# The last attention on tiles of 32 tokens by four heads, with its operands turned through memory

## The reference

```python
q, k, v, gate = jnp.split(proj, [2048, 2048 + 256, 2048 + 512], axis=-1)
q = rope(rms_norm_2(q.reshape(b, s, 32, 64), q_norm_w), pos)
k = rope(rms_norm_2(k.reshape(b, s, 4, 64), k_norm_w), pos)
o = swa_sinks(q, k, v, sinks)      # scale 1/8, keys t-127 .. t, a sink in the softmax
return (o * jax.nn.silu(gate)) @ w_out
```

## Time and profile before

| | us |
|---|---|
| median of 3 runs | 1880.02 (1879.96 to 1880.33) |
| the profiled execution | 1879.77 |
| its span in the trace | 1878.0 |
| PE busy | 1872.9 |
| DVE busy | 1246.1 |
| ACT busy | 991.1 |

### The profile page before, as it was taken

The page is one execution under the profiler, slowest core; times in us unless marked ns, Lnnn a source line. Parts: engine busy times, 40 slices in busy tenths (PEclk is TensorE's granted clock), DMA queues, the critical chain, the costliest instruction groups (busy, mean ns, idle before and its releaser), DMA issues.

```text
span 1878.0 us, 22471 instructions
## 1 busy us (share of the span) xinstructions
PE 1872.9 (100%) x8531; PEld 1543.7 (82%) x8531; DVE 1246.1 (66%) x1861; ACT 991.1 (53%) x1370; POOL 37.6 (2%) x88
## 2 busy tenths in 40 slices
PE   9999999999999999999999999999999999999999
PEld 7888888888888888888888888888888888877777
DVE  6676566776666556665466776765776666777775
ACT  6677554554444344443444455564565555466653
POOL 0001000000000000000000000000000000111100
PEclk9999999999999999999999999999999999999999
DMA  9767764786666666666666696666666677655665
GB/s 324 205 194 179 207 181 152 217 254 196 192 193 194 194 192 191 192 198 192 191 196 195 204 281 196 194 191 190 190 200 194 194 238 235 174 174 175 182 196 171
DMA packets 212363, 375.97 MB, mean 200 GB/s; under 512 B 14672, under 2 KB 35968, under 8 KB 212256
## 3 DMA queue, kind: packets, MB, share of 16 engines
q1 hardware_dynamic: 211008, 371.78, 65.9%
q0 software_dynamic: 816, 2.11, 0.8%
q10 hardware_dynamic: 432, 0.66, 0.1%
HBM read 361.89 MB, written 12.60 MB: 199 GB/s over the span
## 4 chain that ended last, share of the span: by engine, by line
PE 99%; DMA 0%; SPq 0%; DVE 0%; ACT 0%; DVEq 0%; issue 0%
PE g L1225 32%; PE g L1227 32%; PE g L1226 32%; PE m L1159 1%; PE ob L1304 0%; PE m L1286 0%; DMA raw<-in_w_in 0%; PE m L1386 0%; PE m L1284 0%; PE ob L1307 0%; PE m L1271 0%; PE ob L1372 0%; PE m L1316 0%; PE m L1337 0%; PE g L1213 0%; PE g L1212 0%
## 5 line engine op out<-in xcount | busy, mean ns | idle before, releaser
L1696 DVE TENSOR_TENSOR wl<-raw,wh 128x1024 fp32r<-128x1024 f32 (+1 forms) x660 | 802.6, 1217 | 552.7 <-ACT wh L1416 549.4
L1416 ACT ACTIVATE wh<-raw 128x1024 fp32r<-128x1024 f32 (+1 forms) x661 | 695.3, 1053 | 730.9 <-PE g L1227 724.3
L1225 PE MATMUL g<-wh,xh 128*128 128x512 f32 x1886 | 741.1, 393 | 0.3 <-DVE wl L1696 0.3
L1227 PE MATMUL g<-wh,xl 128*128 128x512 f32 x1886 | 734.4, 389 | 0.0
L1226 PE MATMUL g<-wl,xh 128*128 128x512 f32 x1886 | 734.1, 389 | 0.0
L1225 PEld LDWEIGHTS g<-wh,xh 128*128 128x128 f32 x1886 | 354.1, 188 | 78.5 <-issue 3.9
L1227 PEld LDWEIGHTS g<-wh,xl 128*128 128x128 f32 x1886 | 354.0, 188 | 74.0
L1226 PEld LDWEIGHTS g<-wl,xh 128*128 128x128 f32 x1886 | 354.2, 188 | 71.9
L1225 PE MATMUL g<-wh,mh 128*128 128x512 f32 x732 | 287.1, 392 | 0.0
L1227 PE MATMUL g<-wh,ml 128*128 128x512 f32 x732 | 285.0, 389 | 0.0
L1226 PE MATMUL g<-wl,mh 128*128 128x512 f32 x732 | 284.9, 389 | 0.0
(11 more groups left out here) (193 smaller groups left out, 769.5 us busy)
## 6 DMA issues: line engine op xcount, KB each, us to landing
raw<-in_ev_w_in SPq DMA_DIRECT2D x128, 512.0 KB, 3.9
raw<-in_w_in SPq DMA_DIRECT2D x92, 512.0 KB, 4.2
raw<-in_w_gate SPq DMA_DIRECT2D x88, 512.0 KB, 4.4
raw<-in_w_up SPq DMA_DIRECT2D x88, 512.0 KB, 4.3
raw<-in_w_down SPq DMA_DIRECT2D x88, 512.0 KB, 4.6
raw<-in_od_w_in SPq DMA_DIRECT2D x72, 512.0 KB, 4.0
raw<-in_w_out SPq DMA_DIRECT2D x32, 512.0 KB, 4.2
raw<-in_ev_w_out SPq DMA_DIRECT2D x32, 512.0 KB, 4.7
```

Source lines behind the costliest of these rows:

```text
L1225: e.matmul(o, hi[:, kt, c], h, start=first, stop=False)
L1227: last = e.matmul(o, lo[:, kt, c], h, start=False, stop=end)
L1416: return e.activation(o, i, AF.Copy, scale=scale)
L1696: return e.tensor_tensor(o, a, b, op)
```

## The change

The scores are made on tiles of 32 tokens by four heads: 128 rows of the stationary operand are 4 heads x 32 tokens of one chunk, and two such tiles (even and odd heads) lie side by side. A chunk c of the first 128 tokens gets 32c + 32 columns of keys; the chunk c of the other 128 gets the 160 keys from 32c on. A "quad" g is now all eight heads of a key head on the chunks 0 and 3 (g even) or 1 and 2 (g odd) of both halves. To get the queries into this layout, DVE turns blocks of 32 (`qturn`) and SP sends them to memory and fetches them in four DMAs (`qsend`, `qfetch`); the sums' roots go the same way (`rsend`, `rfetch`). The band is added by DVE (`oadd`), the maxima are reductions and are scaled afterwards (`omax`), ACT scales by the root in the exponential, the probabilities are divided by their sum on ACT (`onrm`), turned in blocks of 32 by DVE (`pturn`), sent and fetched back in four DMAs (`psend`, `pfetch`), into tiles that POOL has filled with zeros once. `oapv` has three pairs of matmuls of 256 columns. ACT puts the result into `AW` (`oout`), and the gate, turned as before but without a reciprocal, is multiplied in (`mmul`). The groups of four transposes `oq_turn` and `oapt` are gone. The blocks come as q q g q q g g g, and in the first two blocks of each half of the last projection the units of the lower key tiles come first.

```diff
     block("od_w_in", 0, 2048, 512, every, "X3", "okv")
-    for kind, j in (("oq", 0), ("oq", 1), ("og", 0), ("oq", 2), ("og", 1), ("oq", 3), ("og", 2), ("og", 3)):
+    for kind, j in (("oq", 0), ("oq", 1), ("og", 0), ("oq", 2), ("oq", 3), ("og", 1), ("og", 2), ("og", 3)):
         block("od_w_in", 0, (2560 if kind == "og" else 0) + 512 * j, 512, every, "X3", kind, j)
...
     units[:20] = [un for pair in zip(blocks[0].units, blocks[1].units) for un in pair]
-    for acts, n in (("X1", 12), ("M3", 8), ("X2", 12), ("X3", 12), ("M5", 14)):
+    for acts, n in (("X1", 12), ("M3", 8), ("X2", 12), ("X3", 12), ("M5", 4), ("M5", 12)):
...
-        "ok_dup": (0, .8, 0), "ok_turn": (.6, 0, .45), "oq_turn": (.6, 0, .45), "og": (1.27, 0, 0)}
+        "oqk": (0, 0, 1.2), "oadd": (0, .78, 0), "omax": (0, 1.75, 0), "oexp": (.65, 0, 0), "orec": (0, .36, 0), "onrm": (1.1, 0, 0),
+        "pturn": (0, .85, 0), "oapv": (0, 0, 1.6), "oout": (.8, 0, 0), "mmul": (0, .85, 0),
+        "qturn": (0, .71, 0), "on_sum": (0, 1.2, 0), "on_root": (0, 0, 0), "on_norm": (0, 1.4, 0), "on_rope": (0, 2.15, 0),
+        "ok_dup": (0, .8, 0), "ok_turn": (.6, 0, .45), "og": (1.27, 0, 0)}
 SLOT = 1.36
+CHUNKS = ((0, 3), (1, 2))
+TURNED = (((0, 5), (2, 5), (2, 5), (2, 6)), ((0, 4), (0, 5), (2, 6), (4, 6)))
 
...
         elif kind == "oq":
+            while a[0] and ("qturn", a[0] - 1, 1) not in self.said:
+                yield 1
+            if a[0]:
+                yield from self.made("qturn", a[0] - 1, 1)
             say("oq_evac", a[0], b.i)
-            say("on_sq", a[0])
+            say("on_sq", a[0], 0)
+            while a[0] and ("omax", max(2 * a[0] - 3, 0)) not in self.said:
+                yield 1
             for k in range(2):
                 yield 3 if k else 1
                 yield from self.room("dve", 2.0)
                 say("on_rope", a[0], k)
-            for k, p in enumerate(("on_sum", "on_root")):
-                yield 2 if k else 1
-                yield from self.made("on_rope", a[0], k)
-                say("oq_turn", a[0], k)
-                yield from self.room("dve", 1.0)
-                say(p, a[0])
+                if k:
+                    self.queries_sent(a[0], 0)
+                else:
+                    for i in range(2):
+                        say("on_sum", a[0], i)
+                        if not i:
+                            yield 1
+                            yield from self.made("on_sum", a[0], 0)
+                            say("on_sq", a[0], 1)
+                            yield 1
+                            yield from self.made("on_sq", a[0], 1)
+                            yield from self.room("dve", 1.5)
+                    say("on_root", a[0])
+                    self.spawn(self.roots_sent(a[0]))
+            yield 1
+            self.queries_sent(a[0], 1)
             self.lanes["att"].append(self.od_heads(a[0]))
         else:
             assert kind == "og"
...
+            for g in (2 * a[0], 2 * a[0] + 1):
+                yield 2
+                yield from self.made("og", a[0], b.i)
+                yield from self.room("dve", 1.0)
+                yield from self.turned_and_sent("msent", "M5", 2 * g, "o", g)
 
...
+        yield 1
+
+    def probs_back(self, g):
+
+        yield from self.made("pturn", g, 1)
+        self.say("psend", g)
+        self.end[("psend", g)] = self.now + 5.0
+        yield 4
+        while g >= 2 and ("oapv", g - 2) not in self.said:
+            yield 1
+        self.say("pfetch", g)
+        self.end[("pfetch", g)] = self.now + 8.5
+        yield 1
+
     def fetched(self, p):
 
...
+            yield 1
+        if p[:2] == ("msent", "M5"):
+            yield from self.made("oout", p[4] | 1)
+            yield from self.room("dve", 4.5)
+            self.say("mmul", p[4])
+            yield 1
+            yield from self.made("mmul", p[4])
+            while p[4] and ("msent", "M5", p[2] - 2, "o", p[4] - 1) not in self.said:
+                yield 1
         self.say(*p)
 
...
+        while ("qfetch", g // 2, 1) not in self.said or g and ("oqk", g - 1) not in self.said:
+            yield 1
+        for _ in range(12):
+            if (all(self.end.get(p, 1e9) <= self.now for p in [("qfetch", g // 2, 1)] + self.ring[-3:][:2]) and
+                    self.through["dve"] - self.now <= 4.5):
+                break
+            yield 1
         say("oqk", g)
-        yield 1
-        yield from self.made("oqk", g)
-        yield from self.room("dve", 1.0)
+        for n in range(2):
+            yield 1
...
+        for a in range(2):
+            yield from self.made("onrm", g, a)
+            while g and (("psend", g - 1) not in self.said or self.end[("psend", g - 1)] > self.now):
+                yield 1
+            yield from self.room("dve", 4.5)
+            say("pturn", g, a)
+            yield 1
+        self.spawn(self.probs_back(g))
+        while ("pfetch", g) not in self.said:
+            yield 1
+        for _ in range(12):
+            if self.end[("pfetch", g)] <= self.now:
+                break
+            yield 1
+        for q in (g // 2 * 2 - 2, g // 2 * 2 - 1):
+            while q >= 0 and ("msent", "M5", 2 * q, "o", q) not in self.said:
+                yield 1
+        while g and ("oout", g - 1) not in self.said:
+            yield 1
+        if self.ob:
+            yield from self.made(*self.ob)
         say("oapv", g)
-
-    def od_gate(self, g):
-        while not any(p[:2] == ("og", g // 2) for p in self.said):
-            yield 1
-        yield from self.room("dve", 1.0)
-        self.say("ogate", g)
-        yield 1
-        yield from self.turned_and_sent("msent", "M5", 2 * g, "o", g)
+        yield 2
+        say("oout", g)
 
...
+        def od_chunks(g):
+
+            at = 0
+            for i, c in enumerate(CHUNKS[g % 2]):
+                yield i, c, at, at + 32 * c + 32, at + 32 * c + 192
+                at += 32 * c + 192
 
         def od_scale(g):
...
-                    on.wait_ge(*moved("oq_turn", j, 1))
+                    for k in range(2):
+                        on.wait_ge(s_qback[k], 64 * (j + 1))
                     on.wait_ge(*moved("ok_turn", 1))
-                    for i in (0, 2):
-                        if i == 2:
-                            on.wait_ge(ob_by[ob_free[p][0]], ob_free[p][1])
-                        for n in (0, 1) if i == 0 else (2,):
-                            on.wait_ge(*bank_free("oqk", g, n))
-                        heads = [(od_bank(g, n), qo[rows_of(n), j % 2, 2 * (g % 2) + n // 2, :],
-                                  ko[rows_of(n), j, :]) for n in (i, i + 1)]
-                        for o, q, k in heads:
-                            e.matmul(o[:, 0:128], q[:, 0:128], k[:, 0:128], start=True, stop=True)
-                        for n, (o, q, k) in enumerate(heads):
-                            e.matmul(o[:, 128:384], q[:, 128:256], k[:, 0:256], start=True,
-                                     stop=True).then_inc(s_pv if i + n == 3 else s_bank, 1)
-                elif kind == "oapt":
-                    g, i = a
-                    on.wait_ge(s_oexp, nth("oexp", g, 1 if i == 0 else 3))
-                    on.wait_ge(s_small, 32)
-                    on.wait_ge(*bank_free(*p))
-                    tiles = [(h, c) for h in (2 * i, 2 * i + 1) for c in range(2)]
-                    four(lambda c: bank(*p)[:, 128 * c:128 * c + 128],
-                         lambda c: od_probs(g)[:, tiles[c][0], 128 * tiles[c][1]:128 * tiles[c][1] + 128]).then_inc(s_bank, 1)
+                    for n in range(2):
+                        on.wait_ge(*bank_free(*p, n))
+                    for i, c, at, own, end in od_chunks(g):
+                        for k, lo, hi, key in ((0, at, own, 0), (1, own, end, 32 * c)):
+                            for n in range(2):
+                                last = e.matmul(bank(*p, n)[:, lo:hi], qo[rows_of(n), j % 2, k, c, :],
+                                                ko[rows_of(n), j, key:key + hi - lo], start=True, stop=True)
...
+                    on.wait_ge(s_pback[g % 2], 64 * (g // 2 + 1))
                     on.wait_ge(ob_by[ob_free[p][0]], ob_free[p][1])
                     v = vo[:, :, 64 * (g // 2):64 * (g // 2) + 64]
-                    for i in (0, 2):
-                        for n in (i, i + 1):
-                            e.matmul(OB[rows_of(n), 128 * i:128 * i + 256], v[:, 0, :], od_turned(n)[0],
-                                     start=True, stop=False, skip_group_check=True)
-                        for n in (i, i + 1):
-                            last = e.matmul(OB[rows_of(n), 128 * i + 128:128 * i + 256], v[:, 1, :], od_turned(n)[1],
-                                            start=False, stop=True, skip_group_check=True)
-                    last.then_inc(s_pv, 1)
+                    for k, t, first, last, slots in ((0, 0, True, True, (0, 2)), (1, 0, True, False, (4, 5)),
```

(112 more changed lines are left out.)

349 lines of the change are left out of this document (183 added, 166 removed).

## The result

The changed kernel takes 1891.29 us, median of 4 runs (1889.67 to 1892.46), against 1880.06 us (1879.96 to 1880.33) for the kernel before beside it: a ratio of 1.0060, 95% interval 1.0047 to 1.0072. The forecast was 1866.5 us, with a range up to 1873.0. The direction is wrong, and the size by 25 us.

The account below looks back on a forecast made before the run. PE was taken as the bound, busy 1872.9 of 1878.0 us. Transposes 11.0 and scores 2.6 gave 13.5 us off (rounded), nothing for stalls: 1879.77 - 13.5 + 0.25 = 1866.5 us, range 1864.5 to 1873.0.

Parts of the forecast that it names:

- Transposes: On PE, all oq_turn and oapt groups of four go, 24 at 0.457 us each: 11.0 us saved.
- Scores: On PE, oqk falls from 1.727 to 1.41 us a quad, narrow passes costing as much as 128 columns: 2.6 us saved.
- rival 1: Score passes on PE narrower than 128 columns step by their columns: 1.25 us a quad, 14.8 us off, 1865.2; chance 0.13.
- the estimate that takes the two heads' loads one after the other: Scores on PE with serial loads: 2.16 us a quad, 3.5 us lost there, total gain 7.5, time 1872.5.
- Product with V and the orders: On PE, oapv keeps 768 columns a side and the reordered blocks and units issue the same matmuls: zero change.
- DVE, ACT, the DMA share: Beside PE: DVE at most 17 us more, ACT has 80 us idle, DMA share 0.79 instead of 0.60; no cost.
- PE's new waits: PE waiting for fetched queries and probabilities: 6.7 us at worst; queries short by 0.2, probabilities with 1.8 to spare.
- nothing for stalls: In the final sum, no time was added for PE standing still.
- Rival 2: PE waits for round trips behind other transfers in the queue, a microsecond at each of eight quads: 1874.5; chance 0.17.
- Rival 3: SP's order delays weight loads, PE stands 4.8 us a quad: 1885.7 at four quads, 1904.9 at all eight; chance 0.08.
- The end: Last attention's result ready about 1818 plus 5 us, last projection wants key tiles 12 to 15 at 1825: it fits.

Follow-up runs that it names:

- number 8 alone: Changed kernel, SP as it is, with only the planner's time for the probabilities' outgoing copy set to 8 us instead of 5: 1882.87 us, ratio 1.0017.
- everything together: Changed kernel, all trips on POOL, planner times 8 us for outgoing probabilities, 10 for their fetch, 8 for the first queries' fetch: 1879.75 us, ratio 1.0000.
- 10 for the probabilities: Changed kernel, queries and roots on POOL, planner's 8 us for outgoing probabilities, plus 10 us instead of 8.5 for their fetch: 1874.00 us, ratio 0.9966.
- first experiment: Changed kernel with the planner told 10.5 us instead of 6.5 for the query fetch: 1878.16 us, ratio 0.9992.

## Why the prediction was wrong

- *Transposes, 11.0 us:* right, all 24 groups are gone.
- *Scores, 2.6 us at 1.41 each, against 1.25 by columns:* right, 1.39 to 1.40; rival 1 is out. So is the estimate that takes the two heads' loads one after the other at the price of the Trainium skill, TensorE: Matmul & The Clock Gate, section LDWEIGHTS, which would have shown 2.16.
- *Product with V and the orders, zero:* right, 1.64 to 1.65 and, for the orders, 1.0005 (0.9996 to 1.0015).
- *DVE, ACT, the DMA share:* no term of the sum. DVE was to be busy between nothing and 17 us more and is busy 11 less in the stretch, 4 less in the whole kernel. The mean share came out as forecast (0.78 against 0.79), but the mean hid the stretches near 1 in which the queries travel.
- *"PE's new waits": the step that failed.* "Four issues are 1.85 and a 256 KB return lands in 4.8: 6.7 at worst for either. Queries are short by 0.2", and from it "nothing for stalls". It looks at the second half of the trip, takes medians for a worst case, and takes the copy to leave when the list says so; the first half had its four slots, 5.4 us, against a landing of 4 to 5, elsewhere in the working. What counts is from the copy's slot to the scores, where the list allows 12.2 to 13.8 us. SP was 2 to 6 us behind that slot. The copy landed in up to 6.2 us in the changed kernel and 7.2 in the one with the fetches on POOL (the same 256 KB), and the fetch took 1.9 to issue and 4 to 7 to land (from the last issue's end to PE's start: 4.1 and 7.1 at the first and the fourth pair). Three waits, 14.3 us, stood where the sum had nothing. The row was there: a median of 4.8 at a share of 0.60 is no bound at 0.79 with copies, fetches and 512 KB loads together.
- *Rival 2* named the mechanism, and its chance of 0.17 was too low. Its price, a microsecond at each of eight quads, had the wrong shape: the odd quad of a pair finds its queries there, so three waits of 3.2 to 6.2 us came, no eight of one. Its statement that the queue ahead holds the transfers was half of it; the other half is the issue, which the two kernels with POOL tell apart (13.4 and 1.3 us of waits).
- *Half clock* was in no term. Each of the three waits cost about 2.4 us more than its length (7.1 in all, of which 0.3 each may be the restart), so that 14.3 us of waiting ate 21.4.
- *Rival 3, the weight ring,* didn't happen in the changed kernel: in the stretch ACT never waits for a weight load. Where PE no longer stood still it came in small: ACT waits 4.4 us in two waits with queries and roots on POOL, and 8.3 in four with all trips there. I had asked who waits behind SP's new DMAs, and not what SP's new DMAs wait behind, which are the weight loads. Between SP's free time of 187 us and its being free at the right moment lies the error.
- *The end* held in the changed kernel, but with less to spare than was worked out: 4 us more per query fetch in the list made PE wait 3.2 us for the last key tiles.

## What to carry to other kernels

Where work goes from an engine to a trip through memory, add up the whole trip at loaded durations (the producer's end, the place in an in-order queue behind instructions that wait for something else, copy, issues of the fetch, fetch) and compare it with the distance in the order as it is written; a median landing is no bound. A queue with idle time in sum can still be late at each moment that counts: let the time-critical copy stand on a queue with nothing waiting ahead of it. On a saturated TensorE, price an idle stretch of a few microseconds with the half clock that may follow it (here 2.4 us each time), not by its length alone.

## What the runs showed of the hardware that was not expected

- Behind each of the three waits of PE in the changed kernel (3.15 to 6.23 us) the next matmuls ran at half clock, and so behind 3.09 and 4.36 us (number 8 alone), 3.88 and 5.01 us (everything together). But the wait's length alone doesn't tell it: with the old order of blocks half clock also came behind waits of 2.35 and 1.69 us, while 2.42 us (10 for the probabilities) and 3.16 us (the last key tiles, first experiment) were followed by full speed, with starts 0.23 us apart. What decides was not tried.
- A pass of 32 to 128 columns, two heads side by side, costs what one of 128 does, as far as the sums of a quad show it: scores of 480 instead of 768 columns a side went from 1.727 to 1.40 us, where columns alone would give 1.25 and this floor gives 1.41.
- Kernels in which PE waits for DMAs scatter by 3 to 9 us from run to run, where the kernel before scatters by 0.4 to 1.7. In the kernel with queries and roots on POOL the slower runs are those with the lower mean granted clock.
- A copy issued from POOL takes 0.54 to 0.57 us of its queue, from SP 0.38 to 0.55; four fetches take 2.17 to 2.23 there and mostly 1.80 to 1.89 on SP.
